# Softmax maxima of an attention stage: two small TensorE products and two small steps replaced by a GpSimd mask, one product group and a minimum

## The reference

```python
s = jnp.einsum('bqhd,bkhd->bhqk', q_blk.astype(jnp.float32), kf) * scale
p = jax.nn.softmax(s, axis=-1).astype(v.dtype)
return jnp.einsum('bhqk,bkhd->bqhd', p, v)
```

## Time and profile before

| | |
|---|---|
| median of 3 runs | 4988.72 us (4988.69 to 5009.5) |
| profiled execution | 4992.56 us |
| its span | 4990.8 us |
| granted TensorE clock, mean | 0.976 of 2.4 GHz |
| busy: TensorE, VectorE, ScalarE, GpSimd | 94%, 65%, 41%, 18% |
| attention stages | about 1523 to 2155 us and 4015 to 4655 us of the span |

### The profile page before, as it was taken

How to read it: one execution, slowest core, us unless ns; L and a number is a source line. 1 busy time by engine, 2 the same in 40 slices (tenths; PEclk the granted TensorE clock), 3 DMA queues, 4 the chain that set the end, 5 groups by cost and what they waited for, 6 DMA issues and landing times. The chain is left out here.

```text
span 4990.8 us, 129285 instructions
## 1 busy us (share of the span) xinstructions
PE 4711.4 (94%) x54972; PEld 2930.0 (59%) x54972; DVE 3235.3 (65%) x4928; ACT 2039.0 (41%) x4646; POOL 889.0 (18%) x1230
## 2 busy tenths in 40 slices
PE   8999999989997999989979999999899989999899
PEld 6788444467774544444468884444678745445454
DVE  4555488645666888856545554877466668888565
ACT  1121465445664555521111215554456545555211
POOL 3454000024330000011134440000233300000111
PEclk9999999999999999999999999999999989999999
DMA  5322566456652111155343225664565521111443
GB/s 224 116 100 96 199 209 213 159 159 166 165 143 63 45 30 38 41 173 211 111 156 120 96 98 197 213 217 153 162 173 162 137 61 45 31 37 41 152 169 115
DMA packets 578106, 648.17 MB, mean 130 GB/s; under 512 B 233968, under 2 KB 458736, under 8 KB 567936
## 3 DMA queue, kind: packets, MB, share of 16 engines
q1 hardware_dynamic: 576944, 638.80, 40.9%
q10 hardware_dynamic: 592, 1.10, 0.1%
HBM read 372.64 MB, written 267.13 MB: 128 GB/s over the span
## 5 line engine op out<-in xcount | busy, mean ns | idle before, releaser
L2061 ACT ACTIVATE att_pr<-ps,att_nb 128x512 f32<-128x512 f32 (+1 forms) x960 | 587.9, 621 | 38.2 <-ACT att_nb L2054 1.5
L2384 PE MATMUL ps<-w_out,fin_yT 128*128 128x512 f32 x1280 | 569.8, 599 | 1.3 <-ACT fin_yT L2246 1.3
L2086 DVE TENSOR_REDUCE att_mx<-ps 128x2 f32<-128x1024 f32 (+1 forms) x408 | 488.3, 1197 | 14.2 <-PE ps L1979 14.2
L2108 DVE STREAM_TRANSPOSE att_PT<-att_pr 128x1024 f32<-128x1024 f32 x384 | 469.8, 1223 | 1.9 <-ACT att_pr L2061 1.9
L1979 PE MATMUL ps<-w_out 96*32 96x512 f32 (+1 forms) x3840 | 408.5, 548 | 29.6 <-DMA w_out<-s_qkt 22.2
L2027 PE MATMUL ps<-att_PT,att_V 128*32 128x256 f32 x6144 | 426.4, 391 | 8.5 <-issue 5.7
L1979 PE MATMUL ps<-qk 96*32 96x512 f32 (+1 forms) x3840 | 397.3, 534 | 5.1 <-ACT att_pr L2061 2.7
L2384 PEld LDWEIGHTS ps<-w_out,fin_yT 128*128 128x128 f32 x1280 | 239.2, 192 | 274.2 <-issue 274.2
L598 PE MATMUL ps<-feat_Ts,feat_Ss 128*128 128x256 f32 x1680 | 374.5, 379 | 0.6 <-DVE feat_Ts L502 0.6
L996 PE MATMUL ps<-w_both,prep_hT 128*128 128x512 f32 (+1 forms) x832 | 354.1, 581 | 0.0
L598 PEld LDWEIGHTS ps<-feat_Ts,feat_Ss 128*128 128x128 f32 x1680 | 319.3, 190 | 44.8 <-issue 1.4
(11 more groups left out here) (299 smaller groups left out, 8961.0 us busy)
## 6 DMA issues: line engine op xcount, KB each, us to landing
s_sc<-prep_sc SPq DMA_DIRECT2D x20, 3072.0 KB, 9.0
scan_src<-s_sc SPq DMA_DIRECT2D x104, 384.0 KB, 4.9
s_qkt<-scan_qT SPq DMA_DIRECT2D x40, 576.0 KB
s_zf<-feat_co SPq DMA_DIRECT2D x88, 256.0 KB, 2.5
src<-s_sc SPq DMA_DIRECT2D x56, 384.0 KB, 5.0
s_ht<-feat_hT SPq DMA_DIRECT2D x10, 2048.0 KB, 16.9
s_zt<-st SPq DMA_DIRECT2D x80, 256.0 KB, 3.6
fin_z<-s_zt SPq DMA_DIRECT2D x30, 576.0 KB, 5.4
```

The source lines that it names most:

```text
L2061: last = a.activation(pr[:, m % 4, w * i:w * (i + 1)], ps[:, b0 + w * i // G, w * i % G:w * i % G + w], ACT.Exp, bias=nb[:, m % 2, i:i + 1 ...
L2086: v.tensor_reduce(mx[:, m % 2, 0:n], ps[:, b0:b0 + 2, :].rearrange("p b (u k) -> p (b u) k", u=n // 2), AX.X, ALU.max).then_inc(maxed, 1)
L2108: v.transpose(into, pr[:, m % 4, :].rearrange("p (u k q) -> p u k q", u=n, q=SUB)).then_inc(flipped, 1)
L2384: last = pe.matmul(b, yT[n % TPG][:, k, :], wo[:, k, G * c:G * (c + 1)], start=(k == 0), stop=(k == KD - 1))
```

## The change

The four partial maxima of a query are no longer collected on 32 partitions and spread again. GpSimd multiplies the maxima `mx` (128 x n) by a constant 128 x 4 table that holds minus the scale where the partition lies in strip c and zero elsewhere, into `mm` (128 x 4n): column block c keeps only strip c's maxima. TensorE multiplies this by the `fold` table, once for each column tile, so that every partition gets, in 4n columns of bank 7, the four scaled and negated maxima of its query. VectorE takes their minimum from PSUM straight into `nb`. The turning, the spreading, the cross maximum in `mr` and ScalarE's copy go. On TensorE `fold_max(m - 1)` takes the place of `turn_max(m - 1)`, and the wait for the reciprocals stands ahead of it. The `fold` table is 4 columns wider, and its load is issued before the sample's keys and queries of head 0, since the first mask needs it. One memset goes.

```diff
-    F_SUM, F_TURN, F_SPREAD = 0, QB, QB + 8 * NPART
+    F_SUM, F_MAX = 0, QB
...
-        mr = sb("mr", [P, 2, 2 * TPG])
+        mm = sb("mm", [P, 2, NPART * 2 * TPG])
...
                 load_queries(0, 0, T0, first_in)
                 load_keys(0, 0, T0, first_in)
+                sp.dma_start(fold[:, :], d["consts"][:, K_Q:K_ALL]).then_inc(fold_in, 16)
                 load_keys(0, T0, T, second_in)
                 load_queries(0, T0, T0 + G, second_in)
                 load_queries(0, T0 + G, T, arrived[0])
-                sp.dma_start(fold[:, :], d["consts"][:, K_Q:K_ALL]).then_inc(fold_in, 16)
...
                 def fold_sums(g):
-                    if g == 0:
-                        pe.wait_ge(fold_in, 16)
                     pe.wait_ge(exps, last_chunk[g] + 1)
-                    if g:
-                        pe.wait_ge(inverted, g)
...
-                def turn_max(m):
-                    pe.wait_ge(maxed, m + 1)
-                    n = units_of(m)
+                def fold_max(m):
+                    pe.wait_ge(masked, m + 1)
+                    n = NPART * units_of(m)
                     for c in range(NPART):
-                        last = pe.matmul(ps[0:SUB, BANK_F, F_TURN + n * c:F_TURN + n * (c + 1)], ident[:, SUB * c:SUB * (c + 1)], mx[:, m % 2, 0:n], start=True, stop=True)
-                    last.then_inc(max_turned, 1)
-
-                def spread_max(m, inverted_by_now):
-
-                    pe.wait_ge(crossed, m + 1)
-                    if inverted_by_now:
-                        pe.wait_ge(inverted, inverted_by_now)
-                    n, at_ = units_of(m), F_SPREAD + 8 * (m % 2)
-                    for c in range(NPART):
-                        last = pe.matmul(ps[SUB * c:SUB * (c + 1), BANK_F, at_:at_ + n], ident[:, 0:SUB], mr[:, m % 2, 0:n], start=True, stop=True)
-                    last.then_inc(spread, 1)
+                        last = pe.matmul(ps[SUB * c:SUB * (c + 1), BANK_F, F_MAX:F_MAX + n], fold[:, 0:SUB], mm[:, m % 2, 0:n], start=True, stop=True)
+                    last.then_inc(max_folded, 1)
...
                     if 2 <= m <= NCH + 1:
                         pe.wait_ge(negated, m - 1)
+                    if m and folded_by[m - 1]:
+                        pe.wait_ge(inverted, folded_by[m - 1])
                     for g in folds[m]:
                         fold_sums(g)
                     if 1 <= m <= NCH:
-                        turn_max(m - 1)
+                        fold_max(m - 1)
                     for u in due[m] if m < len(due) else []:
                         weigh(*u)
-                    if 1 <= m <= NCH:
-                        spread_max(m - 1, folded_by[m])
...
+            @block.gpsimd
+            def _(g):
+                def mask_maxima(m):
+
+                    n = units_of(m)
+                    g.wait_ge(maxed, m + 1)
+                    g.tensor_tensor(mm[:, m % 2, 0:NPART * n].rearrange("p (c n) -> p c n", n=n), mx[:, m % 2, 0:n].unsqueeze(1).to_broadcast([P, NPART, n]),
+                                    fold[:, SUB:SUB + NPART].unsqueeze(2).to_broadcast([P, NPART, n]), ALU.mult).then_inc(masked, 1)
+
+                g.wait_ge(fold_in, 16)
+                for m in range(NCH):
+                    mask_maxima(m)
...
-                    a.wait_ge(spread, m + 1)
-                    a.activation(nb[:, m % 2, 0:n], ps[:, BANK_F, at_:at_ + n], ACT.Copy, scale=-SCALE).then_inc(negated, 1)
...
-                v.memset(mr[:, :, :], 0.0).then_inc(zeroed, 1)
...
-                def cross_maxima(m):
+                def negate_maxima(m):
                     n = units_of(m)
-                    v.wait_ge(max_turned, m + 1)
-                    v.tensor_reduce(mr[0:SUB, m % 2, 0:n], ps[0:SUB, BANK_F, F_TURN:F_TURN + n * NPART].rearrange("p (c n) -> p n c", n=n), AX.X, ALU.max).then_inc(crossed, 1)
+                    v.wait_ge(max_folded, m + 1)
+                    v.tensor_reduce(nb[:, m % 2, 0:n], ps[:, BANK_F, F_MAX:F_MAX + n * NPART].rearrange("p (c n) -> p n c", n=n), AX.X, ALU.min).then_inc(negated, 1)
...
+    k[:, K_NS:K_ALL] = np.where(a // SUB == np.arange(P // SUB)[None, :], -DQK ** -0.5, 0.0)
```

More of the change, by code:

```diff
@@ L56 @@
 R_ADAB, R_QKW, R_LNW, R_LNB, R_ALL = np.cumsum([0, 3 * D, 2 * DQK, CW, CW]).tolist()
-K_ID, K_BD, K_MA, K_KX, K_BX, K_RST, K_HS, K_HT, K_Q, K_ALL = np.cumsum(
-    [0, 128, 128, 512, 4 * CH, SUB, 512, BA * (32 * (BA - 1) + HA), P, SUB]).tolist()
+K_ID, K_BD, K_MA, K_KX, K_BX, K_RST, K_HS, K_HT, K_Q, K_NS, K_ALL = np.cumsum(
+    [0, 128, 128, 512, 4 * CH, SUB, 512, BA * (32 * (BA - 1) + HA), P, SUB, P // SUB]).tolist()
 def slot_of(kind, parity):
@@ L1884, in banks_of @@
             return 2 * (m % 3)
-        with stage(nc, "in0 in1 first_in second_in v_in0 v_in1 scored maxed max_turned crossed spread negated exps flipped summed o_out folded inverted normed sent0 sent1 zeroed fold_in chain") as (
-                block, in0, in1, first_in, second_in, v_in0, v_in1, scored, maxed, max_turned, crossed, spread, negated, exps, flipped, summed, o_out, folded, inverted, normed, sent0, sent1, zeroed, fold_in, chain):
+        with stage(nc, "in0 in1 first_in second_in v_in0 v_in1 scored maxed masked max_folded negated exps flipped summed o_out folded inverted normed sent0 sent1 zeroed fold_in chain") as (
+                block, in0, in1, first_in, second_in, v_in0, v_in1, scored, maxed, masked, max_folded, negated, exps, flipped, summed, o_out, folded, inverted, normed, sent0, sent1, zeroed, fold_in, chain):
             arrived, v_in, sent = (in0, in1), (v_in0, v_in1), (sent0, sent1)
@@ L2030, in weigh @@
                         last.then_inc(summed, 1)
-                pe.wait_ge(zeroed, 4)
+                pe.wait_ge(zeroed, 3)
                 for m in range(len(due) + 2):
@@ L2051, in exponentials @@
                     k, n, b0 = group_of(m) % GROUPS, units_of(m), banks_of(m)
-                    at_ = F_SPREAD + 8 * (m % 2)
-                    a.wait_ge(spread, m + 1)
-                    a.activation(nb[:, m % 2, 0:n], ps[:, BANK_F, at_:at_ + n], ACT.Copy, scale=-SCALE).then_inc(negated, 1)
                     if m >= 4:
@@ L2063, in exponentials @@
                     last.then_inc(exps, 1)
-                a.wait_ge(zeroed, 4)
+                a.wait_ge(zeroed, 3)
                 for m in range(2, len(due) + 2):
@@ L2124, in _ @@
                     if 1 <= m <= NCH:
-                        cross_maxima(m - 1)
+                        negate_maxima(m - 1)
                     for g in folds[m]:
```

## The result

The changed kernel takes 4874.53 us (4868.97 to 4882.62, four runs) against 4988.70 before: a ratio of 0.9756, with a 95% interval of 0.9739 to 0.9774.

A forecast was written before the change was run, and what follows sets the result against it. TensorE's instruction stream was taken to bound the regular attention iterations. Savings of 77 - 1 + 3 + 1 = 80 us took the profiled 4992.56 to 4912.6, and the median, 3.8 lower, to 4909 us; range 4893 to 4940.

The forecast's parts named there:

- TensorE's stream is the bound, and its saving comes off each regular iteration: Attention stage, 350 alike iterations: TensorE never without a product; each falls from 2.90 to 2.68 us, 77 us in all.
- Turning 0.22, spreading 0.06, fold 0.06: TensorE, per attention iteration: turning products (0.22 us) and spreading products (0.06) go, one group of four fold products (0.06) comes.
- the flip's smaller margin: First weighing of a group needs its last chunk's flip: margin falls from some 0.24 to 0.11 us; 1 us lost.
- The mask is covered: GpSimd's mask, taken at 0.25 us, hides behind TensorE's scores and weighing, with 0.75 us of slack per iteration.
- VectorE is next in line, at 0.14: VectorE, at its fastest 2.44 us an iteration, would become the bound 0.14 us an iteration further down; not reached.
- ScalarE's copy is worth nothing: Removing ScalarE's 408 copies of the maxima, which lie beside TensorE's work, saves nothing in the regular iterations.
- Heads' starts, 0.1 an iteration, 3 us: 30 iterations at changes of head, paced by exponentials in eight small pieces: 0 to 0.22 us each, taken as 0.1.
- First twelve, 1 us: First twelve iterations of each layer, paced by VectorE or ScalarE: nothing but 1 us for an earlier first exponential.
- Rival 1: VectorE's flip holds GpSimd's mask to its own end: each iteration 0.18 us longer, 63 us slower, 5052; chance 0.09.
- Rival 2: Mask 1.00 us long, or VectorE's lateness after normalisations paid in full: some 0.05 an iteration, 18 us, 4927; chance 0.10.
- Rival 3: TensorE's fold products run one strip behind another, 0.22 us: only the spreading's 0.06 goes, 21 us, 4967; chance 0.05.

The follow-up runs named there:

- masks_6: The changed kernel with each GpSimd mask made six times, each waiting for the one before; measured 5193.3 us.

## Why the prediction was wrong

The direction, the bound and the mechanism were right; the size was not, and a range of 47 us did not hold it. By its own steps:

- **TensorE's stream is the bound, and its saving comes off each regular iteration**: right. It still has no gap, and adding products of either form added their price.
- **Turning 0.22, spreading 0.06, fold 0.06**: the last two right, the first mis-sized. The turning costs 0.25, by the run with four products in one strip. I read the 0.03 by which it starts late as part of the scores, which are 1.72 long and not 1.75. Over 350 iterations that is 10 us; some 3 of them were lost again, where I had said 1 for the flip's smaller margin: the iteration behind each folding of sums is 2.75 instead of 2.65.
- **The mask is covered**: right, 0.20 long and with 0.61 us of slack where I had 0.75. I counted 0.26 from the fold to the minimum, and it is 0.34; from the mask's end to the fold I counted 0.05, and it is 0.15 (`masks_6`).
- **VectorE is next in line, at 0.14**: the 2.44 on which this stands was misread. Those iterations of the kernel before were a ring between two engines and not VectorE at its fastest:

```profile
1549.88 1.90 PE L1979 MATMUL ps<-w_out 96*32 96x512 f32 x16
1551.60 0.39 PE L2000 MATMUL ps<-att_mx,kc 128*32 128x2 f32 x8
1552.03 0.15 DVE L2091 TENSOR_REDUCE att_mr<-ps 32x2 f32<-32x8 f32 x1
1552.24 0.24 PE L2010 MATMUL ps<-att_mr,kc 128*32 128x2 f32 x8 [0.25 <-DVE att_mr L2091]
1552.32 1.90 PE L1979 MATMUL ps<-w_out 96*32 96x512 f32 x16
```

Scores 1.72, turning to maximum 0.43, maximum to spreading 0.21, spreading to scores 0.08: 2.44. L2091 started 0.21 behind the last turning product, as in the earlier trace rows. VectorE's own pace, seen in the changed kernel, is 2.34 or less, so it is farther off than I said.
- **ScalarE's copy is worth nothing**: right in regular iterations, wrong where exponentials set the pace: 0.60 a stretch, 6 us.
- **Heads' starts, 0.1 an iteration, 3 us**: this is the step that failed. They gave 28. 7.3 are the earlier exponentials and the products, and about 20 are stalls of instruction supply that the changed kernel has less of. I had the row that shows it: 16.19 us for three iterations at a clock of 0.68 is no pace of exponentials. I named exponentials and clock and did not ask what the gap ahead of the slow clock was.
- **First twelve, 1 us**: they gave 6.5, and not by chance: both layers' twelve took 74.8 to 77.6 us in the three profiles of the kernel before without a shift and 80.9 in the one with, 67.1 to 70.7 in the eight of the changed one with at most its loads or its placement edited. That the ring of 2.44 is gone is a part of it; the rest was not separated.

The stalls alone don't explain the miss of the range. Without them the change was worth 98.8 us in the attention stages, and 4988.7 less that, 4890, is still 3 us below the range: the turning, the copy and the first twelve make up the rest.

Rival 1 (the flip shuts the mask out) is refuted: masks lie inside flips, 0.20 long, and even with six of them the flips take 1.23 to 1.25 (1.22 to 1.25 before). That is what the Trainium skill, SBUF — State Buffer, section Who interferes with whom, says of a VectorE instruction with at most one SBUF input outside the 2-port modes: it does not contend with GpSimd. Rival 2's mechanism exists and is seen with three masks. Rival 3 is refuted by the 0.06 of the fold.

## What to carry to other kernels

Products of a few columns cost by where they write: four into one column strip 0.25 us, four into four strips 0.06. When a reduction across partitions has to be broadcast again, one constant product per strip on masked data does both at once, and the masking is worth an idle engine only as far as the busy one has no room for it (13 us here). And a gap without a wait behind it deserves a question of its own: large loads issued at the moment a loop changes phase can hold up the instruction supply of the engine that is the bound. Here pieces issued later cost nothing that the runs show, and gave 19 us more.

## What was not expected of the hardware

TensorE's instructions arrive in packets of 16 KB, 256 records' worth, that share the core's 16 DMA engines with the data. Behind 2 MB of loads such a packet came late enough that TensorE, from start to start, had 1.5 to 4.7 us between two products in the two kernels, shifted or not, and it went on 1.2 to 1.7 us after the packet's end in all profiles. During such a gap or within 1.3 us behind it the granted clock fell to 1.2 GHz in six of the ten of the kernel before and in four of the five of the changed one, for 3.4 to 10.2 us (0.68 of full speed as the mean of one stretch). With the queries and keys gone or in pieces no such gap was left at heads 1 to 4, and with the weights in pieces too none at all.

And a gap-free row of an engine is not yet its own pace: L2091's start in the kernel before shows no idle time in its bracket and yet came 0.21 us behind the last turning product, while a VectorE instruction that waited for nothing started 1.16 us behind a flip's start in both kernels (1553.24 to 1554.40 before, 1554.18 to 1555.34 after).
